# Moving columns of the projections read two places in turn, in a two-block transformer kernel on one core

## What is computed

```
for layer in range(2):
    h = rms_norm(x, w)
    proj = h @ w_in                      # 1024 -> 3*512 + 4*512 + 2*256 + 2*512 + 16 + 3*1024
    y_a, y_b, y_c = short_conv(...), retention(...), gated_linear_attention(...)
    merged = (sigmoid(gate_a) * (y_a @ w_branch_a) + sigmoid(gate_b) * (y_b @ w_branch_b)
              + sigmoid(gate_c) * (y_c @ w_branch_c))
    x = x + rms_norm(merged @ w_out)
    x = x + rms_norm(swiglu(rms_norm(x)))          # 1024 -> 2816 -> 1024
x = x + half an FFN;  x = x + attention(...);  x = x + half an FFN
```

## Time and profile before

| | us |
|---|---|
| median of three runs | 2645.31 |
| lowest, highest | 2643.39, 2646.9 |
| span of the profiled execution | 2645.6 |
| TensorE busy in it | 2626.0 |
| VectorE busy | 1914.6 |
| ScalarE busy | 1329.4 |

### The profile page before, as it was taken

How to read it: one execution, slowest core, us unless ns; L and a number is a source line. 1 busy time by engine, 2 the same in 40 slices (tenths; PEclk the granted TensorE clock), 3 DMA queues, 4 the chain that set the end, 5 groups by cost and what they waited for, 6 DMA issues and landing times.

```text
span 2645.6 us, 46776 instructions
## 1 busy us (share of the span) xinstructions
PE 2626.0 (99%) x19468; PEld 2450.8 (93%) x19468; DVE 1914.6 (72%) x2711; ACT 1329.4 (50%) x2008; POOL 57.0 (2%) x59
## 2 busy tenths in 40 slices
PE   9999999999999999999999999999999999999998
PEld 8999999899988999999999998999988977999987
DVE  6956877688854785687778893588944788688943
ACT  5344644465642534654455562455633457456631
POOL 0021000000000003000000000000000000000000
PEclk9999999999999999999999999999999999999999
DMA  4232332333333324233333333233333430233332
GB/s 152 80 106 87 120 99 83 114 120 104 104 106 92 114 80 125 68 120 96 96 119 114 112 96 104 82 120 111 98 103 96 118 104 2 72 120 111 98 108 76
DMA packets 77234, 266.53 MB, mean 101 GB/s; under 512 B 9600, under 2 KB 12032, under 8 KB 76128
## 3 DMA queue, kind: packets, MB, share of 16 engines
q1 hardware_dynamic: 71136, 254.87, 31.1%
q10 hardware_dynamic: 5888, 8.68, 1.3%
HBM read 251.71 MB, written 4.19 MB: 97 GB/s over the span
## 4 chain that ended last, share of the span: by engine, by line
PE 89%; DVE 7%; ACT 2%; issue 1%; DMA 0%; ACTq 0%; DVEq 0%; SPq 0%
PE bank L516 27%; PE bank L517 27%; PE bank L518 27%; PE bank L2064 1%; PE bank L2042 1%; DVE w_lo L704 1%; PE bank L1776 1%; PE bank L2028 1%; DVE w_lo L1242 1%; PE bank L1792 1%; DVE x L870 1%; DVE u_lo L802 1%; DVE acc L816 1%; DVE hid_lo L1345 0%; DVE hid_lo L1347 0%
## 5 line engine op out<-in xcount | busy, mean ns | idle before, releaser
L516 PE MATMUL bank<-u_hi,w_hi 128*128 128x256 f32 (+1 forms) x3120 | 880.3, 282 | 2.0 <-DVE scratch L2603 0.9
L517 PE MATMUL bank<-u_lo,w_hi 128*128 128x256 f32 (+1 forms) x3120 | 869.9, 279 | 0.0
L518 PE MATMUL bank<-u_hi,w_lo 128*128 128x256 f32 (+1 forms) x3120 | 869.8, 279 | 0.0
L516 PEld LDWEIGHTS bank<-u_hi,w_hi 128*128 128x128 f32 x3120 | 587.8, 188 | 11.0 <-issue 4.8
L517 PEld LDWEIGHTS bank<-u_lo,w_hi 128*128 128x128 f32 x3120 | 587.0, 188 | 4.5 <-issue 2.4
L518 PEld LDWEIGHTS bank<-u_hi,w_lo 128*128 128x128 f32 x3120 | 588.2, 189 | 0.7
L704 DVE TENSOR_TENSOR w_lo<-raw,w_hi 128x1024 fp32r<-128x1024 f32 x250 | 311.0, 1247 | 330.8 <-ACT w_hi L700 330.5
L700 ACT ACTIVATE w_hi<-raw 128x1024 fp32r<-128x1024 f32 x250 | 263.3, 1055 | 334.5 <-PE bank L518 255.8
L516 PE MATMUL bank<-cm,w_hi 128*128 128x256 f32 x1152 | 318.0, 276 | 0.0
L517 PE MATMUL bank<-cm,w_hi 128*128 128x256 f32 x1152 | 318.0, 276 | 0.0
L518 PE MATMUL bank<-cm,w_lo 128*128 128x256 f32 x1152 | 318.0, 276 | 0.0
(11 more groups left out here) (358 smaller groups left out, 4372.8 us busy)
## 6 DMA issues: line engine op xcount, KB each, us to landing
raw<-in_weights SPq DMA_DIRECT2D x314, 512.0 KB, 3.5
rx<-in_weights SPq DMA_DIRECT2D x72, 512.0 KB, 3.5
xr<-in_weights SPq DMA_DIRECT2D x48, 512.0 KB, 3.5
raw<-in_weights SPq DMA_DIRECT2D x32, 384.0 KB, 3.0
rot_s<-rot_in ACTq DMA_DIRECT2D x32, 128.0 KB, 2.4
q_s<-q_in ACTq DMA_DIRECT2D x52, 64.0 KB, 2.9
x<-in_x SPq DMA_DIRECT2D x4, 512.0 KB, 6.6
ret_mask<-in_ret_mask SPq DMA_DIRECT2D x2, 1024.0 KB, 6.4
```

What stands on the lines that cost most here:

```text
L516: nc.tensor.matmul(out, st_hi, mv_hi, start=first, stop=False, skip_group_check=onto)
L517: nc.tensor.matmul(out, st_hi, mv_lo, start=False, stop=False, skip_group_check=onto)
L518: return nc.tensor.matmul(out, st_lo, mv_hi, start=False, stop=last, skip_group_check=onto)
```

## The change

Six things change, five of them in the layout of tokens along the free dimension.

1. Each moving operand of `three` (and of the gate-rank matmuls) is read in turn from two places: column 0 of the first half, column 0 of the second, column 1 of the first, and so on (`halves_in_turn`). Where a later use needs halves of 256 tokens to stay apart, the turning is done within each half (`quarters_in_turn`). A result in a bank then holds its tokens interleaved.
2. Where `u` moves in `pe_block`, all 512 columns go in one matmul per part, not two of 256.
3. Takes of a bank read it with a stride of 2 words and write in natural order (`of_halves`, `of_quarters`, `of_half`).
4. Inside an FFN nothing is turned back: `r` is brought into the same order by the fp32 matmul of the sums (`pe_sums_pre`, `ffn=True`), hidden activations stay interleaved, are turned once more by the down projection, and its results are taken with a stride of 4 words (`of_down`).
5. The columns of the value weights are permuted before launch (`value_columns`), so that turned reading gives the natural order.
6. The factor -1 of two gate multiplications leaves them and becomes `scale=-1.0` of the sigmoid; an FFN's last result is taken in two operations of 128 columns for one of 256, the queries `g_q` in two of 256 for one of 512.

Nothing moves past anything else on any queue; semaphores and DMAs are the same.

The core of the diff:

```diff
+        def halves_in_turn(cols):
+            return cols.rearrange("p (h i) -> p i h", h=2)
+        def quarters_in_turn(cols):
+            return cols.rearrange("p (a h i) -> p a i h", a=2, h=2)
+        def by_half(ap):
+            return ap.rearrange("p (h i) -> p h i", h=2)
+        def of_halves(bank):
+            return bank[:, :].rearrange("p (i h) -> p h i", h=2)
+        def of_down(bank):
+            return bank[:, :].rearrange("p (i h a) -> p a h i", a=2, h=2)
...
-            parts = [token_half(0), token_half(1)] if in_hi is u_hi else [slice(0, T)]
...
-                for cols in parts:
-                    mm = three(ps[b][:, cols], w_hi[:, s, w], w_lo[:, s, w], in_hi[:, k0 + k, cols], in_lo[:, k0 + k, cols],
-                               first and k == order[0] and cols.start == 0, last and k == order[-1], cols.start > 0)
+                mm = three(ps[b][:, :], w_hi[:, s, w], w_lo[:, s, w], turns(in_hi[:, k0 + k, :]), turns(in_lo[:, k0 + k, :]),
+                           first and k == order[0], last and k == order[-1])
...
-                            mm = three(to, w_hi[:, slot, w], w_lo[:, slot, w], mv_hi, mv_lo, i < 2 and k == 0, k == KH - 1, i >= 2)
+                            mm = three(to, w_hi[:, slot, w], w_lo[:, slot, w], halves_in_turn(mv_hi), halves_in_turn(mv_lo),
+                                       i < 2 and k == 0, k == KH - 1, i >= 2)
...
-            nc.vector.tensor_scalar(out[:, m, :], use.mem[:, :], gains[:, m:m + 1], None, ALU.mult).then_inc(use.drained, 1)
+            to, of = (by_half, of_halves) if f is None else (by_quarter, of_down)
+            nc.vector.tensor_scalar(to(out[:, m, :]), of(use.mem), gains[:, m:m + 1], None, ALU.mult).then_inc(use.drained, 1)
...
-                        ins = nc.vector.scalar_tensor_tensor(out[:, k, cols], bank, gains[:, k:k + 1], r[:, cols], ALU.mult, ALU.mult)
+                        for bank, to, root in pieces(out[:, k, cols], r[:, cols]):
+                            ins = nc.vector.scalar_tensor_tensor(to, bank, gains[:, k:k + 1], root, ALU.mult, ALU.mult)
...
-                    nc.scalar.activation(gated_s[:, 1, :, :], gated_s[:, 1, :, :], ACT.Sigmoid).then_inc(gate_sig.sem, 1)
+                    nc.scalar.activation(gated_s[:, 1, :, :], gated_s[:, 1, :, :], ACT.Sigmoid, scale=-1.0).then_inc(gate_sig.sem, 1)
...
-                    nc.vector.scalar_tensor_tensor(gated_s[:, 1, :, RIGHT], gated_s[:, 1, :, RIGHT], -1.0, root(RIGHT), ALU.mult, ALU.mult)
+                    nc.vector.tensor_tensor(gated_s[:, 1, :, RIGHT], gated_s[:, 1, :, RIGHT], root(RIGHT), ALU.mult)
...
-                        nc.vector.tensor_tensor(mg_f[:, k, :], ps[4 + n][:, :], g, ALU.mult).then_inc(branch_free[n].sem, 1)
+                        nc.vector.tensor_tensor(by_half(mg_f[:, k, :]), of_halves(ps[4 + n]), by_half(g), ALU.mult).then_inc(branch_free[n].sem, 1)
...
-    return w[:, c:c + T].reshape(KD, P, T).transpose(1, 0, 2).reshape(P, KD * T)
+    in_turn = np.concatenate([np.arange(0, T, 2), np.arange(1, T, 2)])
+    return w[:, c + in_turn].reshape(KD, P, T).transpose(1, 0, 2).reshape(P, KD * T)
```

More of the change, by code:

```diff
@@ L518, in three, with by_quarter, of_quarters, of_half @@
             return nc.tensor.matmul(out, st_lo, mv_hi, start=False, stop=last, skip_group_check=onto)
-        def pe_block(pe, bl, p, ou, e, in_hi, in_lo, k0=0, kn=KD, first=True, last=True, each_k=None, order=None):
+        def halves_in_turn(cols):
[4 more added lines that the diff above has]
+            return ap.rearrange("p (h i) -> p h i", h=2)
+        def by_quarter(ap):
+            return ap.rearrange("p (a h i) -> p a h i", a=2, h=2)
+        def of_halves(bank):
+            return bank[:, :].rearrange("p (i h) -> p h i", h=2)
+        def of_quarters(bank):
+            return bank[:, :].rearrange("p (a i h) -> p a h i", a=2, h=2)
+        def of_down(bank):
+            return bank[:, :].rearrange("p (i h a) -> p a h i", a=2, h=2)
+        def of_half(half):
+            return half.rearrange("p (i h) -> p h i", h=2)
+        def of_down_half(half):
+            return half.rearrange("p (j h g) -> p h g j", h=2, g=2)
+        def down_pieces(bank):
+            turned = of_down_half(bank[:, 0:TH])
+            return lambda to, root: [(turned[:, h], by_quarter(to)[:, h], by_quarter(root)[:, h]) for h in range(2)]
+        def half_pieces(half):
+            return lambda to, root: [(of_half(half), by_half(to), by_half(root))]
+        def pe_block(pe, bl, p, ou, e, in_hi, in_lo, k0=0, kn=KD, first=True, last=True, each_k=None, order=None, turns=halves_in_turn):
             b, s = ou.bank(e), bl.slot(p)
@@ L584, in pe_sums_pre @@
             pe.wait_ge(acc_done.sem, acc_done.upto(s, 7))
[L585 removed]
+            nc.tensor.matmul(use.mem[:, :], ones_c, quarters_in_turn(acc[:, :]) if ffn else acc[:, :], start=True, stop=True).then_inc(use.filled, 1)
         def pe_sums_half(pe, key, s, hf, paired, li=None):
```

113 lines of the change are left out of this document (63 added, 50 removed).

## The result

| | before | after |
|---|---|---|
| median | 2644.70 us (4 runs) | 2558.85 us (4 runs, 2558.3 to 2559.72) |
| ratio | | 0.9673, 95% interval 0.9659 to 0.9686 |
| span of the profiled execution | 2645.6 us | 2557.9 us |

The kernel is 86 us faster; the sum of the forecast was 112 us, its time 2535. The range held the time, the point was 24 us too low. First the page: busy time, and the shares of the last chain (before: the earlier trace rows).

The account below looks back on a forecast made before the run. TensorE, busy 2626.0 of 2645.6 us, was taken as the bound, losing time to stalls fetching moving columns. Terms 31.5 + 9.0 + 37.7 + 36.9 - 3 = 112 us gave 2535 us after rounding up; range 2505 to 2655.

Parts of the forecast that it names:

- 512 columns, 31.5 us for `hid`, `mg`, `y`: 2712 TensorE matmuls already at 512 columns go from 226.6 to 215 ns each through the turns: 31.5 us gained.
- `w`, `u`, gate rank, 9.0 us: 560 matmuls of 512 columns with w, u or ga_w moving go from some 231 to 215 ns: 9.0 us gained.
- 256 columns that stay, 37.7 us: 9744 matmuls still at 256 columns drop from 113.3 to 120 ns to a floor of 111: 37.7 us gained.
- The merge, 36.9 us: 4608 matmuls of u become 2304 of 512 columns, 231 ns a pair to 215 with turns: 36.9 us gained.
- Small change, 3 us: Allowance of 3 us lost on the chain, for late FFN output in two instructions and other small change.
- Strided takes: About 246 VectorE and 60 ScalarE bank reads stepping by 2 or 4 words were taken to cost nothing extra.
- Late output in two pieces: An FFN's result taken in two instructions of 128 columns for one of 256, 8 times: 0 to 3.5 us lost.
- The sign: 24 gate operations lose a factor of -1, which moves into the sigmoid: zero effect.
- D: Rival: strided bank reads cost +0.65 us each and become the bound, 2556 us, or 2657 without a fetch gain (chance 0.06).
- B: Rival: the fetch ignores column order, so distances stay and merge and splits cost a little: 2650 us, chance 0.10.
- The half cure: Rival: the turns remove only part of the fetch stalls, time 2575 to 2640 us, chance 0.10.
- C: Rival: turning breaks the fetch, each column costing up to a second cycle: 4745 us at full price, chance 0.12.

Follow-up runs that it names:

- e3: Kernel before plus 28 groups of 48 matmuls with other column or weight orders behind its last one; 512 columns: 226.7 ns front to back, 215.8 in turn.
- e2: Changed kernel with u again in two matmuls of 256 columns a product, turns kept: 2569.36 us, ratio to before 0.9712.
- e1: Changed kernel with moving columns read front to back again, u still at 512 columns a matmul: 2656.76 us, ratio to before 1.0047.
- e4: Changed kernel with VectorE working out only half the low parts of each weight block from the fifth on: 2539.45 us.
- e5: Kernel before with VectorE working out only half the low parts of each weight block from the fifth on: 2636.64 us.

## Why the forecast was right in kind and 24 us too low

- **What bounds the kernel.** Right: the loss lay in how moving columns are fetched. e3 shows it with nothing but the order changed, 226.7 to 215.8.
- **512 columns, 31.5 us for `hid`, `mg`, `y`.** Measured 226.7 to 215.8, 2712 x 10.9 = 29.6. The floor of 215 from the plain fp32 pass was 0.8 too low.
- **`w`, `u`, gate rank, 9.0 us.** `w` went from 230.7 to 215.8, 480 x 14.9 = 7.2 us, `u` 0.9: about 8.
- **256 columns that stay, 37.7 us.** The floor of 111 from s_diag was 0.7 too low, 6.8 us over 9744. By class over the whole trace: `cm` 113.3 to 111.7, 3456 of them, 5.5 us; `gm` 117.2 to 111.7, 864, 4.8; `hid` and `mg` 119.9 to 111.6, 720, 6.0; the `u` that stays 114.7 to 111.7, 4704, 14.4. Together 30.7, so the floor is the whole of this miss.
- **The merge, 36.9 us.** A pair cost 231.8 in the mean, not 231, and costs 215.8, not 215: 2304 x 16.0 = 36.9, as forecast. Half of it belongs to the turns (231.8 to 223.4, e2), and without them the merge loses (e1), as the prediction said.
- The four rate terms: 115.1 expected, 105.2 measured. This is the smaller part of the miss.
- **Small change, 3 us: the step that failed.** Waits in the three products rose by 15.1 us, the other matmuls by 2.3. I had read VectorE at 72 to 89% busy in its stretches and taken it as beside the matmuls; for the rivals I had even compared its work with TensorE's by stretch (172 us to 168 in the gates), but only for the case in which strided takes cost more. What was not asked is how much slack VectorE had at the places where TensorE meets it when TensorE gets there 4% sooner. e4 and e5 put some 10 of the 15.1 us on VectorE; what the other 5 are stays open. So 3 us stood where 17.4 were measured.
- **Strided takes.** Nothing, as taken: 750 and 681 ns, level with before. Two forms that read a bank and a second tensor with the same stride rose, L2901 from 683 to 821 and L2893 from 688 to 730, 12 x 0.18 = 2.2 us of VectorE. D is out.
- **Late output in two pieces.** 2 x 344 ns for one of 477, 8 times, 1.7 us, inside the 0 to 3.5 given.
- **The sign.** 692 ns with the factor and 692 without: zero.
- **Rivals.** B fell with the first distances. The half cure is out: every class stands at one distance. C is wrong for this kernel's type and right for two others: bfloat16 in turn 484 ns for 216, plain fp32 273 for 216. The Trainium skill, Advanced Engine Details and Errata, SBUF Cachelines, adds to the rule of two hits in one line of 16 bytes that the tolerated stride depends on the type; for bfloat16 and plain fp32 the groups agree with the rule. For fp32r they don't: two places (215.8) should be slow by it, pairs and quads then hop (333 and 250) fast; the measurement decides.

What would have closed some 10 of the 24 us is a second sum, for VectorE: its work from a join to the first products, against TensorE's shortened one.

## What to carry to other kernels

With fp32r operands, read the moving columns in turn from two places that each march on, at least 4 columns apart (hops of just 4 want a start on a multiple of 4): 512 columns stand 215.8 ns apart for 226.7 to 234, at every start tried (216.6 for one of 2 columns on). Don't do it with bfloat16 or plain fp32, and don't use more places than two. A result in turned order costs nothing to take out with a stride of 2 or 4 words, unless a second input is strided too; but once TensorE is faster, look for the engine that was just in time: here a sixth of the gain at the array went back, more than half of that by VectorE, and neither meeting it later nor lending it GpSimd helped. And read the granted clock beside every distance, since a group at 0.50 looks like a price of its order.

## What the runs showed of the hardware that I had not expected

- The same order of reading gains 5% in fp32r, costs 27% in plain fp32 and 124% in bfloat16 (226.7 to 215.8, 215.9 to 273.2, 216 to 484.4).
- Front to back, a start moved by 8 columns (32 bytes) against the weights costs 6.7 ns per 512 columns; in turn the place doesn't matter.
- The weights' load doesn't tolerate a stride: 128 columns at 111.6 ns, 118 with every 2nd weight column, 233 with every 4th; 512 in turn go from 215.8 to 241.5 with every 8th.
- 64 moving columns cost as much as 128 (112 ns). At a granted clock of 0.50 they take 213, front to back and in turn alike.
- One addition on GpSimd beside VectorE at a join holds single VectorE operations up by as much as 1.08 us, and 18 additions that save VectorE 12 us make the kernel 21 us slower, in part through TensorE's clock, which fell to 0.50 after waits of 1.9 us.
